# Two norms of a two-layer transformer step: 1/rms moved behind the products, and the first half of three layers' weights split a stage ahead

## What is computed

```python
def rms_norm(x, gain):           # x * rsqrt(mean(x^2) + 1e-6) * gain, over the 1024 features
    ...
# even layer, after the attention
hp = hp + merge_even(o_a, o_b, w_out_even)                    # 1024 -> 1024, added to the residual
hp = hp + swiglu(rms_norm(hp, norm_ffn_even), w1_ffn, w3_ffn, w2_ffn)
def swiglu(xn, w1, w3, w2):      # 1024 -> 2816, 2816 -> 1024
    return jnp.einsum('btf,fd->btd', jax.nn.silu(xn @ w1) * (xn @ w3), w2)
# odd layer: the input projection, 1024 -> 4624, cut into q, f, i, g, z, xbc, dt
proj = jnp.einsum('btd,de->bte', rms_norm(hp, norm_mix_odd), w_in)
# silu(q), sigmoid(f), silu(g), silu(z), a causal convolution over xbc, softplus(dt + bias)
```

## Time and profile before

| | |
|---|---|
| median of 3 runs | 1611.05 us (1608.66 to 1612.43) |
| profiled execution: time | 1612.39 us |
| profiled execution: span of the trace | 1610.3 us |
| mean granted TensorE clock | 0.992 of full speed |
| TensorE busy | 1575.6 us, 98% |
| VectorE, ScalarE busy | 511.0 us, 32%; 367.5 us, 23% |
| output projection | 187.57 to 219.99 us |
| feed-forward up, down | 224.33 to 371.2, 371.5 to 451.2 us |
| odd layer's input projection | 451.5 to 578.2 us |
| experts | from about 714.75 us |

### The profile page before, as it was taken

The page is one execution under the profiler, slowest core; times in us unless marked ns, Lnnn a source line. Parts: engine busy times, 40 slices in busy tenths (PEclk is TensorE's granted clock), DMA queues, the critical chain, the costliest instruction groups (busy, mean ns, idle before and its releaser), DMA issues.

```text
span 1610.3 us, 37445 instructions
## 1 busy us (share of the span) xinstructions
PE 1575.6 (98%) x16871; PEld 1009.6 (63%) x16871; DVE 511.0 (32%) x723; ACT 367.5 (23%) x594; POOL 43.9 (3%) x50
## 2 busy tenths in 40 slices
PE   9989899999999999999999999999999999999997
PEld 8976699999999986683353443533534435435344
DVE  6456555543367757743201101101011011011113
ACT  4236344333245747420000000000000000000001
POOL 0000000000000000000010000000000000000000
PEclk9999999999999999999999999999999999999999
DMA  9566426444425462559999999999999999999996
GB/s 354 186 220 206 133 91 197 157 158 156 154 88 192 174 141 88 147 218 417 374 390 408 416 411 416 416 411 415 414 412 413 411 417 416 409 417 414 408 412 236
DMA packets 144488, 479.46 MB, mean 298 GB/s; under 512 B 32184, under 2 KB 61632, under 8 KB 129747
## 3 DMA queue, kind: packets, MB, share of 16 engines
q1 hardware_dynamic: 141404, 469.08, 75.8%
q0 software_dynamic: 2064, 5.66, 0.9%
q10 hardware_dynamic: 871, 2.42, 0.4%
HBM read 463.57 MB, written 13.55 MB: 296 GB/s over the span
## 4 chain that ended last, share of the span: by engine, by line
PE 53%; DMA 2%; DVE 1%; ACT 0%; issue 0%; SPq 0%; DVEq 0%
PE ps L2973 36%; PE ps L2989 16%; DMA down_ring<-in_we_dram 1%; DMA xn_tokens<-y_rows 1%; PE ps L3038 0%; DVE act L3174 0%; DVE act L3179 0%; PE ps L3017 0%; PE ps L2998 0%; PE ps L3023 0%; PE ps L3005 0%; DVE act L3197 0%; DVE tail_rows L3179 0%; DVE act L3187 0%; DVE tail_rows L3187 0%
## 5 line engine op out<-in xcount | busy, mean ns | idle before, releaser
L2973 PE MATMUL ps<-up_ring,item_x 128*32 128x448 f32 x6000 | 565.6, 539 | 0.0
L2973 PEld LDWEIGHTS ps<-up_ring,item_x 128*32 128x32 f32 x6000 | 195.6, 110 | 364.8 <-issue 363.6
L2989 PE MATMUL ps<-down_ring,hid_t 128*32 128x256 f32 x5376 | 291.8, 379 | 0.4 <-DMA down_ring<-in_we_dram 0.4
L2989 PEld LDWEIGHTS ps<-down_ring,hid_t 128*32 128x32 f32 x5376 | 175.2, 110 | 118.1 <-issue 3.9
L3159 DVE TENSOR_TENSOR hid<-hid,ps 128x1344 f32<-128x1344 f32 x16 | 24.9, 1554 | 652.1 <-PE ps L2973 650.7
L3238 ACT COPY item_y<-ps 128x512 f32<-128x512 f32 x8 | 4.7, 586 | 422.8 <-PE ps L2989 422.8
L1583 PE MATMUL ps<-x_hi_up,w_hi_up 128*128 128x288 f32 x320 | 86.1, 299 | 0.1
L1584 PE MATMUL ps<-x_lo_up,w_hi_up 128*128 128x288 f32 x320 | 86.0, 295 | 0.0
L3234 ACT ACTIVATE hid<-ps 128x1344 f32<-128x1344 f32 x16 | 20.7, 1292 | 261.1 <-PE ps L2973 239.9
L547 PE MATMUL ps<-x_hi_in_odd,w_hi_in_odd 128*128 128x288 f32 x256 | 69.6, 297 | 0.0
L548 PE MATMUL ps<-x_lo_in_odd,w_hi_in_odd 128*128 128x288 f32 x256 | 69.5, 297 | 0.0
(11 more groups left out here) (522 smaller groups left out, 1948.3 us busy)
## 6 DMA issues: line engine op xcount, KB each, us to landing
up_ring<-in_we_dram SPq DMA_DIRECT2D x250, 896.0 KB, 11.1
down_ring<-in_we_dram SPq DMA_DIRECT2D x112, 1024.0 KB, 13.8
ring<-in_w_ffn_dram SPq DMA_DIRECT2D x23, 1024.0 KB, 5.8
ring<-in_w_in_odd_dram SPq DMA_DIRECT2D x9, 2048.0 KB, 7.8
ring<-in_w_in_even_dram SPq DMA_DIRECT2D x5, 2048.0 KB, 15.9
ring<-in_w_ffn_dram SPq DMA_DIRECT2D x5, 2048.0 KB, 7.7
ring<-in_w_out_odd_dram SPq DMA_DIRECT2D x3, 2048.0 KB, 9.4
odd_layer<-in_we_dram SPq DMA_DIRECT2D x6, 896.0 KB, 13.3
```

What stands on the lines that cost most here:

```text
L2973: mm = pe.matmul(k.ps[32 * q:32 * q + 32, 3 * w + g, 0:FW], xg[:, c, g, :], block_of[:, q, :], start=c == 0, stop=c == DC - 1, skip_group_ ...
L2989: mm = pe.matmul(k.ps[32 * q:32 * q + 32, 6 + g // 2, 256 * (g % 2):256 * (g % 2) + 256], hidT[:, 2 * r + j, g, :], block_of[:, j, 256 * q ...
```

## The change

`Norm`, `Squares` and `gemm` are removed. Both norms become `LateNorm`; the first of the three places is the feed-forward, the second the input projection.

- **Output projection** (`stage_out_even`, new): half 0 is rounded in four pieces, in turn with the four pairs of input chunks; its rest is taken in two pieces; three warm-ups instead of six. As each residual chunk is added (all but the last), ScalarE rounds it times the gain and VectorE takes its rest. The next stage's weight half 0 is rounded and its rest taken here too.
- **Feed-forward up**: TensorE starts on the ready half; the eighth chunk is split at the stage's start. Squares, fold and roots run beside steps 0 to 2, and the sum matmul follows step 1. Per step, VectorE multiplies both tiles by 1/rms into SBUF (`scale`, two instructions that were not there before), then silu, product, rounding, rest (`Hidden`). The down stage's half 0 is made here. The last step's gate work moves into the down stage.
- **Feed-forward down**: starts without warm-up on a ready half. The first half of the input projection is rounded here, and six of the eight residual chunks are split here.
- **Input projection**: TensorE starts on chunks 0 to 5; all 37 tiles leave through VectorE times 1/rms, and the 16 gated ones get their silu on ScalarE from SBUF. Block order is changed so that the ungated v comes last. The dt product uses the residual with weights times gain. Convolutions are at groups 7, 8, 9, 11, 13, 15 (before 7 to 12), the f gate's arithmetic at 12 (before 11).

All weights and activations of the touched stages lie in buffers shared by the four stages at the other end of SBUF. The core of the diff:

```diff
-IN_ODD_BLOCKS = (6, 7, 8, 9, 1, 0, 2, 3, 4, 5)
+IN_ODD_BLOCKS = (6, 7, 8, 9, 1, 0, 3, 4, 5, 2)
 class LateNorm:
+    def take_chunk(self, dve, c, x):
+        dve.wait_ge(*self.rounded.at(self.lead + c + 1))
     def await_chunk(self, pe, c):
-        pe.wait_ge(*self.rest.at(c + 1))
+        if self.lead + c >= 0:
+            pe.wait_ge(*self.rest.at(self.lead + c + 1))
 def gemm_rows(...):            # the down stage
-                k.warm(pe, 7, 3 if norm else 6)
+                if norm:
+                    k.warm(pe, 7, 3)
...
+                        if hidden and h == 0 and m == 2 * ((total - 1) % 4):
+                            pe.wait_ge(*hidden.scaled.at(2))
...
-                if not head:
-                    squares.sums(pe)
...
+                if late:
+                    sp_.round_hi(act, last + 1)
+                    for m in range(in_time):             # in_time = 6
                         act.wait_ge(*added.at(m + 1))
-                        squares.square(act, m)
+                        late.round_chunk(act, m, k.residual[:, m, :])
...
+                    if late and 1 <= m <= in_time:
+                        late.take_chunk(dve, m - 1, k.residual[:, m - 1, :])
+def stage_out_even(k, x, weights, norm):
...
+            n = DC // PIECES
+            for p in range(PIECES):
+                x.round_pair(act, p)
+                act.copy(sp_.view(sp_.hi, 0)[:, n * p:n * p + n, :], halves[0][2][:, n * p:n * p + n, :]).then_inc(...)
+            act.preload_act_table_set(LOG_EXP)
+            sp_.round_hi(act, 1)
+            for h in range(len(halves)):                 # 4 halves and the next stage's first
+                sp_.round_hi(act, h + 2)
+                for m in (2 * h, 2 * h + 1):
+                    if m < LAST:
+                        act.wait_ge(*added.at(m + 1))
+                        norm.round_chunk(act, m, k.residual[:, m, :])
+class Hidden:
+    def scale(self, dve, m):
+        for w in range(2):
+            dve.tensor_tensor(self.pair[m % 2][:, w, :], self.bank(m, w), self.norm.rstd[:, :], ALU.mult)
+    def gate(self, act, m):      # silu in place, after the first scale
+    def multiply(self, dve, m):  # after the gate and the second scale
+    def round(self, act, m): ...
+    def take(self, dve, m): ...
 def stage_ffn_up
+            norm.round_chunk(act, DC - 1, k.residual[:, DC - 1, :])
+            sp_.round_hi(act, 1)
+            norm.square(act)
+            sp_.round_hi(act, 2)
+            norm.roots(act)
+            for m in range(FC - 1):
+                if m >= 1:
+                    sp_.round_hi(act, m + 2)
+                hidden.gate(act, m)
+                hidden.round(act, m)
...
+            for m in range(FC - 1):                      # VectorE
+                if m >= 1:
+                    sp_.take_lo(dve, m + 2)
+                dve.wait_ge(*done.at(m + 1))
+                hidden.scale(dve, m)
+                if m >= 1:
+                    hidden.take(dve, m - 1)
+                hidden.multiply(dve, m)
 def stage_in_odd
+                    for j, p in enumerate(group):
+                        if p == SUM:                     # SUM = 6
+                            pe.wait_ge(*norm.mean.at(1))
                         if p >= 7:
-                            pe.wait_ge(*place(p - 7))
+                            pe.wait_ge(*out[1].at(p - 6))
...
+            def leave(dve, p):
...
+                    return dve.tensor_tensor(proj[:, m, :], bank[:, 0:T], rstd[:, :], ALU.mult)
...
+                    if len(group) == 2:                  # ScalarE, ahead of the silus now
+                        sp_.round_hi(act, half + 2)
+                    if g == 0:
+                        norm.roots(act)
+                    for p in group:
+                        if p in gated:
+                            act.wait_ge(*out[1].at(p + 1))
+                            act.activation(one, one, ACT.Silu)
```

More of the change, by code:

```diff
@@ new lines, with __init__, bank, nth @@
+class Hidden:
+    def __init__(self, k, s, parts, norm):
+        self.k, self.parts, self.norm = k, parts, norm
+        self.pair = [k.sb(s, f"hidden_pair{n}", [P, 2, T]) for n in range(2)]
+        self.done, self.scaled, self.gated, self.made = (k.count(n) for n in ("pair_done", "scaled", "gated", "hidden_made"))
+        self.rounded, self.rest, self.before = k.count("rounded"), k.count("rest"), 0
+    def bank(self, m, w):
+        return self.k.ps[:, 2 * (m % 4) + w, 0:T]
+    def nth(self, m):
+        return m + 1 - self.before
+    def scale(self, dve, m):
+        for w in range(2):
+            dve.tensor_tensor(self.pair[m % 2][:, w, :], self.bank(m, w), self.norm.rstd[:, :], ALU.mult).then_inc(*self.scaled.up())
+    def gate(self, act, m):
+        one = self.pair[m % 2][:, 0, :]
+        act.wait_ge(*self.scaled.at(2 * self.nth(m) - 1))
+        act.activation(one, one, ACT.Silu).then_inc(*self.gated.up())
+    def multiply(self, dve, m):
+        one, other = (self.pair[m % 2][:, w, :] for w in range(2))
+        dve.wait_ge(*self.gated.at(self.nth(m)))
+        dve.wait_ge(*self.scaled.at(2 * self.nth(m)))
+        dve.tensor_tensor(other, one, other, ALU.mult).then_inc(*self.made.up())
+    def round(self, act, m):
+        act.wait_ge(*self.made.at(self.nth(m)))
+        act.copy(self.parts[0][:, m, :], self.pair[m % 2][:, 1, :]).then_inc(*self.rounded.up())
+    def take(self, dve, m):
+        dve.wait_ge(*self.rounded.at(self.nth(m)))
+        dve.tensor_tensor(self.parts[1][:, m, :], self.pair[m % 2][:, 1, :], self.parts[0][:, m, :].bitcast(F32), ALU.subtract)\
+           .then_inc(*self.rest.up())
@@ L1705, in _ @@
             def _(pe):
-                sp_.start_products(pe, norm, x, [[sp_.tile(k.ps[:, 2 * h + j, 0:T], h, j) for j in range(2)] for h in range(2)], [[done] * 2] * 2)
-                pe.wait_ge(*past_in.at(16))
-                for c in range(CC):
-                    mm = pe.transpose(k.ps[:, 7, 24 * c:24 * c + 24], old[:, P * c:P * c + P], k.const("ident")[0:24, 0:24])
-                mm.then_inc(*past_turned.up())
-                half = 2
-                for group in IN_ODD_GROUPS[2:]:
+                tiles = [sp_.tile(k.ps[:, j, 0:T], 0, j) for j in range(2)]
@@ new lines, in _ @@
+                for c in range(DC):
+                    norm.await_chunk(pe, c)
+                    for to, hi, _ in tiles:
+                        pe.matmul(to, hi(c), x[0][:, c, :], start=c == 0, stop=False)
+                        pe.matmul(to, hi(c), x[1][:, c, :], start=False, stop=False)
+                sp_.await_lo(pe, 0)
+                for to, _, lo in tiles:
+                    for c in range(DC):
+                        mm = pe.matmul(to, lo(c), x[0][:, c, :], start=False, stop=c == DC - 1)
+                    mm.then_inc(*done.up())
@@ L1714, in _ @@
+                half = 1
+                for g, group in enumerate(IN_ODD_GROUPS[1:], 1):
+                    if g == 2:
+                        norm.sum(pe, SUM)
+                        pe.wait_ge(*past_in.at(16))
+                        for c in range(CC):
+                            mm = pe.transpose(k.ps[:, 7, 24 * c:24 * c + 24], old[:, P * c:P * c + P], k.const("ident")[0:24, 0:24])
+                        mm.then_inc(*past_turned.up())
                     for j, p in enumerate(group):
+                        if p == SUM:
+                            pe.wait_ge(*norm.mean.at(1))
@@ L1786, in extra @@
                         silu(2 * (g - 12) + 1)
-                norm.roots(act, sp_)
+                for c in range(HELD, DC):
+                    norm.round_chunk(act, c, k.residual[:, c, :])
+                sp_.round_hi(act, 1)
+                norm.square(act)
                 half = 0
                 for g, group in enumerate(IN_ODD_GROUPS):
-                    for p in group:
-                        if p in on_act:
-                            act.wait_ge(*done.at(p + 1))
-                            leave(act, p).then_inc(*out[0].up())
                     if len(group) == 2:
```

500 lines of the change are left out of this document (215 added, 285 removed).

## The result

| | before | changed |
|---|---|---|
| median of four runs | 1610.98 us (1608.66 to 1612.43) | 1592.77 us (1589.23 to 1597.92) |
| profiled execution: time, span | 1612.39, 1610.3 us | 1589.23, 1587.0 us |
| mean granted clock of it | 0.992 | 0.993 |

The ratio is 0.9891, 95% interval 0.9861 to 0.992: faster by 1.1%, some 18 us. Forecast were 1584.6 and a range up to 1591.5, so the direction was right, the size was missed by 8.2 us, and the range by 1.3.

What follows compares the result with a forecast made beforehand. TensorE was taken to set the pace before the experts, transfers being full only there, with losses at handoffs. Gains 4.6 + 6.6 + 6.4 + 6.5 + 2.4 = 26.5 from 1611.05 gave 1584.6 us, range 1580.5 to 1591.5.

Steps and rivals of the forecast that it cites:

- Term 1: Start of the output projection: pieces interleaved, lo products of the first tiles end at 8.6 instead of 13.22; gain 4.6 us.
- Term 2: Output projection to up: 20.9 us shrinks to 14.3, with 1.0 idle; gain 6.6 us, bounds 5.0 and 7.3.
- TensorE waits for the last add (0.45 from 220.19) ... 1.0 us idle: Output projection to up: after the last add and a 0.3 us barrier TensorE resumes at about 221.0, 1.0 us idle.
- The up stage's ring: Feed-forward up: the loop of rounding, rest, scales, product takes 6.15 us a step, so TensorE's 6.4 wins by 0.25.
- The rival from the Trainium skill's "VectorE: DVE Perf Modes", section "The DRAIN you can't avoid": Feed-forward up: VectorE instructions never overlap, so the ring takes 6.6 us, costing 3.2 us, total 1587.8; chance 0.06.
- Term 3: Up to down: 6.99 us at clock 0.76 becomes 0.6 idle without warm-up; gain 6.4 us, bounds 4.8 and 6.7.
- Terms 4 and 5: Down to input projection, 20.8 to 14.3 us, gain 6.5; inside the input projection, waits vanish as rounding stands first, gain 2.4.
- The clock at bare handoffs: Rival: the clock falls at handoffs without warm-ups, 1.6 us each at one to four places, 1586.2 to 1591.0; chance 0.08.
- Nothing is later than it was to the experts ... they shift whole: Experts: their first transfers are issued by the stages before, so they start earlier by the whole 26.5 us saved.
- the sign of being wrong: Experts: the prediction is wrong if their window grows by what the stages save.
- The experts' window unchanged: Experts: their window, 885.25 us from 714.75 us before, keeps its length, listed among the signs of being right.
- four falls of the clock and term 5 at nothing: Lower bound of all terms: gains 2.9, 5.0, 4.8 and 4.9, sum 17.6 us, total 1593.5.

Runs made afterwards that it cites:

- run 7: Changed kernel with chunk 6 also rounded and rested at the start of up, so the last add comes first: 1589.61 us (four executions), before 1610.53.
- run 10: run 7's kernel plus warm-ups filling idles at the second recurrent stage's end and the odd output projection's start: 1586.13 us (six executions).
- run 8: Changed kernel with ScalarE's rounding of the next weight half put behind the silus from the input projection's third group on: 1578.76 us.
- run 9: Changed kernel without an edit on a third chip: median 1584.88 us of five executions, before 1609.41; ratio 0.9851.
- run 3: Changed kernel with GpSimd's gathers of the next item's rows held back until seven down blocks were used: 1595.85 us.
- run 2: Kernel before, without an edit, profiled again on the chip that also repeated the changed kernel: 1612.22 us (13 executions), the profiled one 1622.08.
- runs 1 to 4: One chip: changed kernel unedited (1590.12 us), kernel before unedited (1612.22), changed kernel with gathers held back (1595.85), changed kernel with warm-ups put back (1600.32).
- runs 7 to 12: Six traces with gathers on two other chips: five of the changed kernel, unedited or edited, and one of the kernel before, unedited (1606.83 us).
- run 4: Changed kernel with six warm-up matmuls put back at the start of up, down and input projection: 1600.32 us (ten executions).

## Why the prediction was right and wrong

- **Term 1** (4.6): from the warm-up to the third tile 15.22 less 10.73, 4.5, in the first pair, 3.1 with a steady clock. Mechanism right; the 1.6 of clock was there in two of four executions.
- **Term 2** (6.6): the stretch to up gave 10.0, 5.5 of it here. The step "TensorE waits for the last add (0.45 from 220.19) ... 1.0 us idle" failed: I took the add from the old queue, and the change puts a rest that waits for ScalarE ahead of it. Measured 1.75; run 7, which takes that rest away, gives back 0.93.
- **The up stage's ring**: right. 142.05 us from up to down, no wait. The rival from the Trainium skill's "VectorE: DVE Perf Modes", section "The DRAIN you can't avoid", would have made the ring 6.6 and the stage 3.2 longer. The trace doesn't agree: 22 x 6.4 + 0.5 + 0.67 is 141.97, measured were 142.05. The prediction took from that section the sentence that the next instruction waits until the pipe is empty, and left out what stands behind it, that an instruction that isn't held starts earlier; so page and trace need not differ.
- **Term 3** (6.4): 6.35 in the first pair, 4.7 with a steady clock (146.7 or 146.8 to 142.05). I had written that the clock was at 0.76 there and counted all of it. At the two places of terms 1 and 3 the kernel before has a fall in two of four traces, the changed one in none of ten; so few traces don't show whether the change keeps the clock up or merely met none.
- **Terms 4 and 5** (6.5 + 2.4): 7.56 + 1.99 in the first pair. Down to input projection takes 77.2 to 78.6 before (four traces) and 70.3 to 72.4 after; about 6.0. The spread between like kernels is even over the stage, at a clock of 1.00 and without a wait: 48 matmuls take 6.24 us in run 10, 6.32 in run 8 and 6.45 in run 9, and why is open. The gap before the input projection was 1.2 to 1.4 where 1.0 was forecast. Inside the input projection 2.0, in all traces. Its size was right, its reason not: run 8 shows that the order of roundings and silus is not what removed the waits. That the 21 exits left ScalarE, or that blocks and convolutions come in another order, remains as the cause, by argument only.
- **The clock at bare handoffs**: no fall there in eight of nine traces of kernels without the warm-ups. In run 3 it fell 0.6 us after the gap of 1.76, and up took 1.7 longer, so the rival exists at the price that it had, at one place in one trace:

```profile
214.83:217.00 2.17, 2.17 (x11) 2.17 (x12) 0.52 (x1) 2.17 (x2) 0.00 (x0) 0.63 0.00 0
217.00:220.40 3.40, 3.40 (x21) 3.40 (x20) 3.23 (x2) 2.26 (x3) 0.00 (x0) 0.73 0.00 0
```

- **"Nothing is later than it was to the experts ... they shift whole"**: they do. The experts' code loses nothing by the change; the kernel before loses the same, 8.8 us for 8.9, where there is a hole. The window did grow in the first pair, which the prediction had named as the sign of being wrong; run 2 shows that this sign could not tell the change from the execution.

So three things in the sum failed. Terms 1 and 3 counted 1.6 us each of a fallen clock, 3.1 measured, as if every execution had it: two of four traces of the kernel before do. Term 2 missed a wait, that of the last add behind a rest, 0.9. Terms 4 and 5 were together 1.0 too large. This leaves 21.5 of 26.5 with a steady clock and some 24.6 with both falls; paired measurements gave 22.1, 24.5 and, without gathers, 20.3.

At a steady clock that is 5.0 of the 8.2 us missed, as an estimate. For the other 3.3 the sum had no term: two executions differ in code that nobody touched. "The experts' window unchanged" is true of the kernel but not of these executions: the base has a trace without a hole, the changed kernel's profiled execution has one, at a net price of 4.1 us. For the unprofiled executions there is only their clock: the four of the changed kernel have 1578.8 us of span x clock in the mean, between the 1574.0 of the chip without holes and the 1583.5 of the chip with them. How much of the 3.3 is the hole stays an estimate.

On a chip without holes the changed kernel's median is 1584.9, at the forecast's 1584.6. That is luck in part: the base is 1.6 lower there, and these executions had the better clock. And the range was narrower than its own bounds: four falls of the clock and term 5 at nothing gave 1593.5, which would have held the 1592.77, but the range ended at 1591.5.

## What to carry to other kernels

Before a stall at a handoff goes into the sum, look at the granted clock in it, and count its clock share only as often as other executions have it. A stage that takes over work at its end needs the last instruction of each queue checked anew: what the old trace says of the last add holds only while nothing that waits stands ahead of it. Cut the traces of both kernels at the same places first; what moved in code that nobody touched is the measure of what two single executions can tell.

## What the runs showed of the hardware

- Beside GpSimd's gathers TensorE's weight loads stop in the middle of a stream with nothing to wait for, mostly twice by about 0.5 us, which lengthens an item by 0.7 to 1.8 us: in every item that has gathers in five traces (the changed kernel's first, and runs 1 to 4 on one chip), in none in seven others (the kernel before's first, and runs 7 to 12 on two more chips). A start of 14 us later moves the hole along.
- The granted clock falls to 1.2 GHz at places that differ between executions of one kernel: from none before the last 4 to 6 us (0.998 and 0.999) to a mean of 0.986. On one chip the kernel before ran 1601.8 us of span at 0.997 and 1616.6 at 0.989. The places come again, only not in every execution: in the 13 us before the experts' first product the clock falls in 11 of 14 traces, at the first products of the output projection in 2 of the 4 of the kernel before.
- A warm-up did not cover the barrier ahead of its stage: 1.75 us idle, then 3.15 of warm-up (run 4).
